# Regrouping the attention steps of a one-core decoder layer: probabilities times v one step later

## The chip, the cores and the metric

One core of one Trainium2 chip runs the whole layer as one program. The metric is the device time of an execution in microseconds; lower is better. The engines have short names here: PE is TensorE (its weight loads are PEld), DVE is VectorE, ACT is ScalarE, POOL is GpSimd, and SP is the queue that issues most transfers.

## What is computed

One decoder layer on a sequence of 512 rows and 1024 channels, all in 32-bit floats. Only the attention half of the first sub-layer matters here, with what stands right behind it:

```python
proj = rms_norm(h, mix_pre_g) @ w_in          # q, k, v, u, gv: 5 x 512 columns
attn_out = moba_attention(q, k, v)            # 8 heads x 64; with 512 rows all past blocks are selected: causal attention
gmlp_out = gmlp_spatial_gating(gelu(u), gelu(gv), ...)
mixed = concat([rms_norm(attn_out, attn_out_g), rms_norm(gmlp_out, gmlp_out_g)])
h = h + rms_norm(mixed @ w_o, mix_post_g)
hn = rms_norm(h, mlp_pre_g)                   # then w_up, squared relu, w_down, and the gated embedding
```

## The kernel before

The rows are cut into four tiles of 128 (`qt`, or `t`). Every large product is made of three matmuls in fp32r (high by high, high by low, low by high), so each weight slab and each activation is split into a high part by ACT (`w_hi`, line 935) and a low part by DVE (`w_lo`, line 440). A projection tile `proj(n)` is 24 matmuls of 512 columns in one PSUM bank. There is no planner: each engine runs a list that is written out by hand, and semaphores order the lists.

The attention runs in 16 steps, four row tiles times four pairs of heads; unit 4*qt + pair is one pair of one row tile. In a step PE does this, in this order:

1. `scores(step)`: six matmuls in fp32r, two heads side by side on 64 rows of the array each (lines 1607, 1611, 1612 with kT), into banks 3 and 4. It waits until ACT has read the scores of the step before (`probs_ready`).
2. `turn_probs(step - 1)`: full-array transposes of the probabilities (line 1754) into banks 5 and 6, qt + 1 for each head.
3. half a projection tile, 12 matmuls (lines 1607, 1611, 1612 with actT or mixT). Steps 4 and 5 make the two halves of tile 19 (v of the last rows); from step 6 on they are tiles of the output projection, whose second halves (the attention rows) wait for `attn_lo`.
4. `attend(step - 1)`: probabilities times v in plain fp32, two heads side by side on 64 columns of the array each (line 1774), into bank 7. It waits until DVE (`drain_pt0`, line 557) and ACT (`drain_pt1`, line 1073) have copied the transposes out.

Meanwhile DVE masks the scores, takes the maxima (`row_maxima`, lines 543, 548, 551) and copies out head 0; ACT does the exponentials (`softmax`, line 1064) and copies out head 1. In steps 0 to 2 and 5 to 8 both also split two weight slabs (`STEP_SPLITS`), and in steps 1, 3 and 5 ACT drains a tile of v (`proj_drain`, line 1021).

When a row tile is complete, a chain of small operations normalises it:

- `attn_inverse` (DVE, lines 564, 566): reciprocal of the row sums, spread over 512 columns of `attn`
- `turn_inverse` (PE, line 1661), `drain_inverse` (ACT, line 1078): transposed, and back into `attn`
- `attn_columns` (DVE, line 573): times bank 7
- `square_attn` (ACT, line 1086), `attn_sum` (DVE, line 578), `mean_square` (PE, line 1700, one column), `attn_mean` (DVE, line 583)
- one power on POOL (line 1454), `attn_spread` (DVE, line 588), `turn_scale` (PE, line 1705, in the middle of the projection), `attn_scale` (DVE, line 595), `attn_hi` (ACT, line 1090) and `attn_lo` (DVE, line 602)

Before the change the first three and the square stand in step 4*qt + 4, the sum and the mean in step 4*qt + 5, and the rest in step 4*qt + 6. The mean is written to bank 7.

Behind the last step come the remaining output projection (tiles 25 to 27), the residual (`add_mixed(t)`: DVE, two of line 615 and two of line 623), the square of the new h (`square_h1(t)`, ACT, line 969), its root on POOL (lines 1387, 1388), `norm_h1(t)` (ACT, line 1113) and the transposes `turn_hn` (PE, line 1661) for the MLP. Here ACT and DVE also split the four slabs of `w_ple` (lines 933 and 437) and then the first slabs of `w_up`. The raw slabs pass through a ring of two pairs: SP issues the load of a pair (line 1532) when DVE has made the low parts of the pair two before it. ACT's list there is: `square_h1(2)`, the split of the first `w_up` pair, `norm_h1(2)`, `square_out(3)`, the second pair, `hn_turn_hi(4)` and `(5)`, `square_h1(3)`, the third pair, `norm_h1(3)`; PE's `turn_hn(6)` waits for the last. PE's program for the whole layer is one fixed list too: what it loses in a wait is made up nowhere.

Of the kernel before, what the change touches and what calls it, by code (L numbers as in the profile page):

```python
# [39 lines left out]
P = 128  # L40
D = 1024
SEQ = 512
TT = SEQ // P
KD = D // P
W = 512
# [9 lines left out]
EPS = 1e-6  # L55
# [58 lines left out]
def phase_one_results():  # L114

    names = []
    for n in range(20):
        names.append(("proj", n))  # L120
        if n in (8, 9):
            names += [("mix", 2 * (n - 8)), ("mix", 2 * (n - 8) + 1)]
        if 9 <= n <= 16:
            names.append(("qkT", n - 9))
        if 12 <= n <= 15:
            names.append(("gateT", n - 12))
    names += [("proj", n) for n in range(20, 26)]
    first = {"proj": 0, "mix": BANK_S, "qkT": BANK_PT, "gateT": BANK_O}
    turns = {"proj": 3, "mix": 2, "qkT": 2, "gateT": 1}
    banks = {(kind, i): first[kind] + i % turns[kind] for kind, i in names}  # L130

    banks["proj", 3], banks["proj", 4], banks["proj", 5] = BANK_S, BANK_S + 1, BANK_PT
    a, b, c = (banks["proj", n] for n in (20, 21, 22))
    late = [(("attnT", 0), b), (("proj", 19), c), (("proj", 20), a), (("attnT", 1), c), (("proj", 21), b),
            (("proj", 22), c), (("attnT", 2), b), (("proj", 23), a), (("proj", 24), b),
            (("hT", 0), 5), (("hT", 1), 6), (("attnT", 3), 4), (("proj", 25), c), (("hT", 2), a), (("hT", 3), 6),
            (("proj", 26), 3), (("proj", 27), 4),
            (("ple", 0), 7), (("ple", 1), 6), (("ple", 2), 5), (("hT", 4), a), (("hT", 5), b),
            (("ple", 3), c), (("ple", 4), 7), (("ple", 5), 6), (("hT", 6), 3),
            (("hT", 7), 4), (("ple", 6), 5), (("ple", 7), a)]  # L140
    assert c == banks["proj", 19]
    banks.update(late)
    return names[:-7] + [name for name, _ in late], banks


def tail_results():
# [33 lines left out]
def hymba_layer(nc, x, xT, pT, weights, columns, rope, ws, rows, out):  # L180
# [6 lines left out]
    with ExitStack() as ctx:  # L187
# [237 lines left out]
        def _(dve):  # L425
# [154 lines left out]

            def attn_mean(qt):
                dve.wait_ge(mean_filled, qt + 1)
                nc.vector.tensor_scalar(mean_at[:, qt:qt + 1], psum[:, BANK_O, W - P:W - P + 1], EPS, None,
                                        ALU.add).then_inc(mean_ready, 1)

            def attn_spread(qt):
# [43 lines left out]
                        bank1["hT", i])  # L630

            for step in range(TT * PAIRS):
                if step >= 6 and step % 4 == 2:
                    attn_spread(step // 4 - 1)
                row_maxima(step)
                if step >= 1:
                    drain_pt0(step - 1)
                if step >= 4 and step % 4 == 0:
                    attn_inverse(step // 4 - 1)
                if step >= 5 and step % 4 == 1:  # L640
                    attn_sum(step // 4 - 1)
                if step >= 6 and step % 4 == 2:
                    attn_scale(step // 4 - 1)
                if step >= 6 and step % 4 == 2:
                    attn_lo(step // 4 - 1)
                for slab in STEP_SPLITS.get(step, ()):
                    splits(slab)
                if step >= 4 and step % 4 == 0:
                    attn_columns(step // 4 - 1)
                if step >= 5 and step % 4 == 1:  # L650
                    attn_mean(step // 4 - 1)
                if step == 11:
                    add_mixed(0)
                if step == 15:
                    add_mixed(1)
            drain_pt0(15)
            attn_inverse(3)
            hn_turn_lo(0)
            hn_turn_lo(1)
            attn_columns(3)  # L660
# [4 lines left out]
            hn_turn_lo(3)  # L665
            attn_scale(3)
            attn_lo(3)
            for i in range(2):
                splits(SLAB_PLE + 2 * i)
            add_mixed(2)  # L670
            dve.wait_ge(pT_hi_done, 1)
            nc.vector.tensor_tensor(pT_lo[:], pT_raw[:], pT_hi[:].bitcast(F32), ALU.subtract
                                    ).then_inc(pT_lo_done, 1)
# [250 lines left out]
        def _(act):  # L924
# [194 lines left out]


            for step in range(TT * PAIRS):
                if step >= 1:
                    drain_pt1(step - 1)
                softmax(step)
                if step >= 6 and step % 4 == 2:
                    attn_hi(step // 4 - 1)
                for slab in STEP_SPLITS.get(step, ()):
                    splits(slab)
                if step in (1, 3, 5):
                    proj_drain(17 + step // 2)  # L1130
                if step == 10:
                    square_out(0)
                if step == 12:
                    square_h1(0)
                    norm_h1(0)
                if step >= 4 and step % 4 == 0:
                    drain_inverse(step // 4 - 1)
                    square_attn(step // 4 - 1)
                if step == 14:
                    square_out(1)  # L1140
            drain_pt1(15)
            square_h1(1)
            hn_turn_hi(0)
            hn_turn_hi(1)
            norm_h1(1)
            drain_inverse(3)
            square_attn(3)
            act.wait_ge(pv_done, 16)
            act.dma_start(pT_raw[:], pT).then_inc(pT_loaded, 16)
# [451 lines left out]
        def _(pe):  # L1601
# [95 lines left out]

            def mean_square(qt):
                pe.wait_ge(at_summed, qt + 1)
                nc.tensor.matmul(psum[:, BANK_O, W - P:W - P + 1], at_rows[:], mean_of_w[:],  # L1700
                                 start=True, stop=True).then_inc(mean_filled, 1)

            def turn_scale(qt):
# [42 lines left out]
            def turn_probs(unit):  # L1746

                qt = unit // PAIRS
                pe.wait_ge(probs_ready, unit + 1)
                if unit == 0:  # L1750
                    pe.wait_ge(*drained["qkT", 2 * TT - 1])
                for s in range(2):
                    for k in range(qt + 1):
                        mm = nc.tensor.transpose(psum[:, BANK_PT + s, k * P:(k + 1) * P],  # L1754
                                                 probs[:, unit % 2, s, k * P:(k + 1) * P], ident[:])
                    mm.then_inc(pt_filled, 1)
# [20 lines left out]
                mm.then_inc(pv_done, 1)  # L1777

            for step in range(TT * PAIRS):
                scores(step)  # L1780
                if step >= 1:
                    turn_probs(step - 1)
                n, k0 = STEP_TILES[step]
                proj(n, range(k0, k0 + 2))
                if step in (6, 10, 14):
                    turn_scale(step // 4 - 1)
                proj(n, range(k0 + 2, k0 + 4))
                if step in (4, 8, 12):
                    turn_inverse(step // 4 - 1)
                if step >= 1:  # L1790
                    attend(step - 1)
                if step in (5, 9, 13):
                    mean_square(step // 4 - 1)
            turn_probs(15)
            proj(25, range(0, 4))
            pe.wait_ge(pt0_drained, TT * PAIRS)
            pe.wait_ge(pt1_drained, TT * PAIRS)
            turn_hn(0)
            turn_hn(1)
            turn_inverse(3)  # L1800
            attend(15)
            proj(25, range(4, 8))
            mean_square(3)
            turn_hn(2)
# [195 lines left out]
```

## Time and profile before

| | us |
|---|---|
| median of 3 runs (lowest, highest) | 615.1 (615.03, 616.13) |
| profiled execution, whole time | 614.93 |
| its span, first to last instruction | 613.2 |
| PE busy in the span | 600.3 (98%) |
| DVE, ACT, POOL busy | 403.8, 313.2, 82.5 |

The profiled execution lies 0.2 us under the median, and 1.7 us of it lie outside the span. A matmul of 512 columns is shown 0.39 us long, but the next one starts 0.23 us after it: they are pipelined, and their ends are modelled. So distances on PE are read from start to start. The attention steps run from about 109 to 190 us, and the MLP begins behind 222 us.

### The profile page before, as it was taken

Reading aid. Unit: us, or ns where it says so; the run is one execution under the profiler, and the core shown is the slowest. Engines: PE = TensorE matmul, PEld = TensorE weight load, DVE = VectorE, ACT = ScalarE, POOL = GpSimd, SP = SyncE. Lnnn points to the kernel's source line nnn. Section 1 sums busy time; section 2 is a strip of 40 time slices with the busy share of each in tenths; the row PEclk is TensorE's granted clock in tenths of the full one; section 3 lists DMA queues with packets and bytes.
Section 4 is the critical chain, followed back from the end, with each engine's and each line's share of the span. In section 5 each row is a group of like instructions: output and inputs, shape, how many; then the busy total and the mean of one; then the engine's idle time right before and its main releaser. Section 6 shows DMA issues by size and latency. Waiting matters only on the chain.

```text
span 613.2 us, 7823 instructions
## 1 busy us (share of the span) xinstructions
PE 600.3 (98%) x2922; PEld 489.4 (80%) x2922; DVE 403.8 (66%) x603; ACT 313.2 (51%) x541; POOL 82.5 (13%) x152
## 2 busy tenths in 40 slices
PE   8999999999999999999999999999999999999995
PEld 6888888777767878888888888888888888888884
DVE  5476444567755793766867757757778578668654
ACT  6754544656454755554534625544546355534422
POOL 1176332000001120001001001010010010001011
PEclk9999999999999999999999999999999999999998
DMA  8654332223000359554737556638365566234011
GB/s 309 253 195 141 105 103 69 68 69 104 1 2 26 110 181 322 139 210 93 190 137 158 137 156 153 220 75 201 138 134 145 160 151 210 93 130 168 13 69 69
DMA packets 23653, 82.90 MB, mean 135 GB/s; under 512 B 2752, under 2 KB 3136, under 8 KB 23104
## 3 DMA queue, kind: packets, MB, share of 16 engines
q1 hardware_dynamic: 18000, 60.83, 28.2%
q0 software_dynamic: 4032, 14.68, 14.0%
q10 hardware_dynamic: 1584, 6.90, 2.9%
q8 instruction: 23, 0.38, 0.2%
q14 instruction: 14, 0.11, 0.1%
HBM read 78.20 MB, written 4.19 MB: 134 GB/s over the span
## 4 chain that ended last, share of the span: by engine, by line
PE 88%; DVE 5%; ACT 3%; issue 1%; DMA 1%; POOL 1%; SPq 0%; DVEq 0%; ACTq 0%; POOLq 0%
PE psum L1607 28%; PE psum L1612 28%; PE psum L1611 28%; PE psum L1661 2%; PE psum L1774 1%; PE psum L1754 1%; DVE stat L548 1%; DMA first_raw_a<-weights_dram 1%; DVE w_lo L440 1%; ACT work L1113 1%; PE psum L1675 1%; ACT probs L1064 1%; ACT w_hi L935 0%; DVE psum L615 0%; DVE psum L543 0%
## 5 line engine op out<-in xcount | busy, mean ns | idle before, releaser
L440 DVE SCALAR_TENSOR_TENSOR w_lo<-raw,cols,w_hi 128x512 fp32r<-128x512 f32 x112 | 86.3, 813 | 46.7 <-ACT w_hi L935 46.5
L1612 PE MATMUL psum<-actT_hi,w_lo 128*128 128x512 f32 x256 | 99.8, 390 | 0.0
L1611 PE MATMUL psum<-actT_lo,w_hi 128*128 128x512 f32 x256 | 99.8, 390 | 0.0
L1607 PE MATMUL psum<-actT_hi,w_hi 128*128 128x512 f32 x256 | 99.7, 389 | 0.0
L935 ACT ACTIVATE w_hi<-raw,cols 128x512 fp32r<-128x512 f32 x112 | 74.3, 713 | 42.8 <-PE psum L1607 25.4
L1607 PE MATMUL psum<-w_hi,actT_hi 128*128 128x512 f32 (+1 forms) x232 | 90.6, 390 | 1.3 <-DVE w_lo L440 1.2
L1612 PE MATMUL psum<-w_hi,actT_lo 128*128 128x512 f32 (+1 forms) x232 | 88.7, 383 | 0.0
L1611 PE MATMUL psum<-w_lo,actT_hi 128*128 128x512 f32 (+1 forms) x232 | 88.7, 382 | 0.0
L1607 PE MATMUL psum<-t_hi,a_hi 128*128 128x512 f32 x212 | 83.6, 394 | 0.0
L1611 PE MATMUL psum<-t_lo,a_hi 128*128 128x512 f32 x212 | 83.6, 394 | 0.0
L1612 PE MATMUL psum<-t_hi,a_lo 128*128 128x512 f32 x212 | 83.6, 394 | 0.0
L764 DVE TENSOR_TENSOR acc<-acc,psum 128x512 f32<-128x512 f32 x90 | 58.4, 682 | 22.6 <-PE psum L1612 22.4
L1611 PEld LDWEIGHTS psum<-actT_lo,w_hi 128*128 128x128 f32 x256 | 48.1, 188 | 10.4
L1607 PEld LDWEIGHTS psum<-actT_hi,w_hi 128*128 128x128 f32 x256 | 48.1, 188 | 10.3
L1612 PEld LDWEIGHTS psum<-actT_hi,w_lo 128*128 128x128 f32 x256 | 48.0, 188 | 10.1
L1472 POOL DMA_DIRECT2D raw_x<-weights_dram x21 | 18.5, 883 | 259.4 <-DVE t_lo L705 259.4
L705 DVE TENSOR_TENSOR t_lo<-raw_x,t_hi 128x1024 fp32r<-128x1024 f32 x28 | 34.3, 1224 | 27.1 <-ACT t_hi L1195 27.1
L1607 PEld LDWEIGHTS psum<-w_hi,actT_hi 128*128 128x128 f32 x232 | 43.6, 188 | 10.2 <-DVE w_lo L440 1.9
L1612 PEld LDWEIGHTS psum<-w_hi,actT_lo 128*128 128x128 f32 x232 | 43.6, 188 | 8.6
L1611 PEld LDWEIGHTS psum<-w_lo,actT_hi 128*128 128x128 f32 x232 | 43.7, 188 | 7.9
L1195 ACT ACTIVATE t_hi<-raw_x 128x1024 fp32r<-128x1024 f32 x28 | 29.6, 1057 | 36.7 <-DMA raw_x<-weights_dram 27.2
L1612 PEld LDWEIGHTS psum<-t_hi,a_lo 128*128 128x128 f32 x212 | 39.8, 188 | 9.3
(169 smaller groups left out, 917.8 us busy)
## 6 DMA issues: line engine op xcount, KB each, us to landing
raw<-weights_dram SPq DMA_DIRECT2D x66, 512.0 KB, 3.6
raw_o<-weights_dram SPq DMA_DIRECT2D x23, 512.0 KB, 4.0
raw_x<-weights_dram POOLq DMA_DIRECT2D x21, 512.0 KB, 5.4
raw_x<-weights_dram SPq DMA_DIRECT2D x9, 512.0 KB, 5.4
raw_o<-weights_dram POOLq DMA_DIRECT2D x7, 512.0 KB, 9.0
ple_spill<-ple ACTq DMA_DIRECT2D x1, 2048.0 KB, 9.4
out_dram<-h SPq DMA_DIRECT2D x7, 256.0 KB, 2.0
xT_raw<-xT_dram SPq DMA_DIRECT2D x4, 256.0 KB, 5.8
```

The lines of the kernel that those rows point to most:

```text
L440: nc.vector.scalar_tensor_tensor(out=w_lo[:, place_at, :], in0=source, scalar=gain, in1=high, op0=ALU.mult, op1=ALU.subtract).then_inc(sla ...
L548: nc.vector.tensor_reduce(row_max, psum[:, BANK_S:BANK_S + 2, 0:n], AXIS_X, ALU.max).then_inc(max_found, 1)
L705: nc.vector.tensor_tensor(t_lo[n % T_RING][:], t_source(n), t_hi[n % T_RING][:].bitcast(F32), ALU.subtract).then_inc(t_lo_done, 1)
L764: nc.vector.tensor_tensor(part, part, bank, how).then_inc(product_added, 1)
L935: nc.scalar.activation(w_hi[:, place_at, :], source, ACT.Copy, scale=gain).then_inc(slab_hi, 1)
L1064: last = nc.scalar.activation(probs[:, unit % 2, s, 0:n], psum[:, BANK_S + s, 0:n], ACT.Exp, bias=neg_max[:, s:s + 1], scale=SCALE, accum_ ...
L1195: nc.scalar.activation(t_hi[n % T_RING][:], t_source(n), ACT.Copy).then_inc(t_hi_done, 1)
L1472: nc.gpsimd.dma_start(raw_x[step % 2][:], weights[down_in_stream(step, rows, half)], accum_op=ALU.add).then_inc(x_added, 16)
L1607: begin = nc.tensor.matmul(out, a_hi, b_hi, start=first, stop=False, skip_group_check=read_between)
L1611: nc.tensor.matmul(out, a_hi, b_lo, start=False, stop=False, skip_group_check=read_between)
L1612: return nc.tensor.matmul(out, a_lo, b_hi, start=False, stop=last, skip_group_check=read_between)
L1661: mm = nc.tensor.transpose(psum[:, banks[name], j * P:(j + 1) * P], source[:, j * P:(j + 1) * P], ident[:])
```

## The change

PE does `attend` for the unit two steps back, between the scores and the transposes, instead of for the last unit behind the projection. `turn_inverse` moves from the end of step 4*qt + 4 to the middle of step 4*qt + 5, between `attend` and `turn_probs`. `mean_square` moves from the end of step 4*qt + 5 to step 4*qt + 6, between the scores and `attend`; for the first three row tiles it now writes to column 0 of bank 5, and waits until DVE has read the transposes there; `turn_probs` in the same step waits until the mean is read. On ACT `drain_inverse` goes to the head of step 4*qt + 5, and `square_attn` behind the softmax, the splits and the `proj_drain` of that step. On DVE `attn_columns` and `attn_sum` are in step 4*qt + 5, and `attn_mean` stands ahead of the maxima of step 4*qt + 6. Behind the steps, `attend(15)` and `turn_inverse(3)` change places on PE, `drain_inverse(3)` goes ahead of `norm_h1(1)` on ACT, `attn_inverse(3)` ahead of `drain_pt0(15)` on DVE, and `add_mixed(2)` ahead of the splits of `w_ple` on DVE.

```diff
--- before.py
+++ after.py
@@ -141,6 +141,10 @@
     assert c == banks["proj", 19]
     banks.update(late)
     return names[:-7] + [name for name, _ in late], banks
+
+
+def mean_bank(qt):
+    return BANK_PT if qt < TT - 1 else BANK_O
 
 
 def tail_results():
@@ -580,7 +584,7 @@
 
             def attn_mean(qt):
                 dve.wait_ge(mean_filled, qt + 1)
-                nc.vector.tensor_scalar(mean_at[:, qt:qt + 1], psum[:, BANK_O, W - P:W - P + 1], EPS, None,
+                nc.vector.tensor_scalar(mean_at[:, qt:qt + 1], psum[:, mean_bank(qt), 0:1], EPS, None,
                                         ALU.add).then_inc(mean_ready, 1)
 
             def attn_spread(qt):
@@ -630,31 +634,31 @@
                         bank1["hT", i])
 
             for step in range(TT * PAIRS):
-                if step >= 6 and step % 4 == 2:
-                    attn_spread(step // 4 - 1)
+                qt, turn_of = step // 4 - 1, step % 4 if step >= 4 else -1
+                if turn_of == 2:
+                    attn_mean(qt)
                 row_maxima(step)
+                if turn_of == 2:
+                    attn_spread(qt)
                 if step >= 1:
                     drain_pt0(step - 1)
-                if step >= 4 and step % 4 == 0:
-                    attn_inverse(step // 4 - 1)
-                if step >= 5 and step % 4 == 1:
-                    attn_sum(step // 4 - 1)
-                if step >= 6 and step % 4 == 2:
-                    attn_scale(step // 4 - 1)
-                if step >= 6 and step % 4 == 2:
-                    attn_lo(step // 4 - 1)
+                if turn_of == 0:
+                    attn_inverse(qt)
+                if turn_of == 1:
+                    attn_columns(qt)
+                if turn_of == 2:
+                    attn_scale(qt)
+                    attn_lo(qt)
                 for slab in STEP_SPLITS.get(step, ()):
                     splits(slab)
-                if step >= 4 and step % 4 == 0:
-                    attn_columns(step // 4 - 1)
-                if step >= 5 and step % 4 == 1:
-                    attn_mean(step // 4 - 1)
+                if turn_of == 1:
+                    attn_sum(qt)
                 if step == 11:
                     add_mixed(0)
                 if step == 15:
                     add_mixed(1)
+            attn_inverse(3)
             drain_pt0(15)
-            attn_inverse(3)
             hn_turn_lo(0)
             hn_turn_lo(1)
             attn_columns(3)
@@ -665,9 +669,9 @@
             hn_turn_lo(3)
             attn_scale(3)
             attn_lo(3)
+            add_mixed(2)
             for i in range(2):
                 splits(SLAB_PLE + 2 * i)
-            add_mixed(2)
             dve.wait_ge(pT_hi_done, 1)
             nc.vector.tensor_tensor(pT_lo[:], pT_raw[:], pT_hi[:].bitcast(F32), ALU.subtract
                                     ).then_inc(pT_lo_done, 1)
@@ -1119,6 +1123,8 @@
 
 
             for step in range(TT * PAIRS):
+                if step >= 5 and step % 4 == 1:
+                    drain_inverse(step // 4 - 1)
                 if step >= 1:
                     drain_pt1(step - 1)
                 softmax(step)
@@ -1133,8 +1139,7 @@
                 if step == 12:
                     square_h1(0)
                     norm_h1(0)
-                if step >= 4 and step % 4 == 0:
-                    drain_inverse(step // 4 - 1)
+                if step >= 5 and step % 4 == 1:
                     square_attn(step // 4 - 1)
                 if step == 14:
                     square_out(1)
@@ -1142,8 +1147,8 @@
             square_h1(1)
             hn_turn_hi(0)
             hn_turn_hi(1)
+            drain_inverse(3)
             norm_h1(1)
-            drain_inverse(3)
             square_attn(3)
             act.wait_ge(pv_done, 16)
             act.dma_start(pT_raw[:], pT).then_inc(pT_loaded, 16)
@@ -1697,7 +1702,9 @@
 
             def mean_square(qt):
                 pe.wait_ge(at_summed, qt + 1)
-                nc.tensor.matmul(psum[:, BANK_O, W - P:W - P + 1], at_rows[:], mean_of_w[:],
+                if qt < TT - 1:
+                    pe.wait_ge(pt0_drained, 4 * qt + 5)
+                nc.tensor.matmul(psum[:, mean_bank(qt), 0:1], at_rows[:], mean_of_w[:],
                                  start=True, stop=True).then_inc(mean_filled, 1)
 
             def turn_scale(qt):
@@ -1749,6 +1756,8 @@
                 pe.wait_ge(probs_ready, unit + 1)
                 if unit == 0:
                     pe.wait_ge(*drained["qkT", 2 * TT - 1])
+                if unit >= 5 and unit % 4 == 1:
+                    pe.wait_ge(mean_ready, unit // 4)
                 for s in range(2):
                     for k in range(qt + 1):
                         mm = nc.tensor.transpose(psum[:, BANK_PT + s, k * P:(k + 1) * P],
@@ -1777,28 +1786,30 @@
                 mm.then_inc(pv_done, 1)
 
             for step in range(TT * PAIRS):
+                qt, turn_of = step // 4 - 1, step % 4 if step >= 4 else -1
                 scores(step)
+                if turn_of == 2:
+                    mean_square(qt)
+                if step >= 2:
+                    attend(step - 2)
+                if turn_of == 1:
+                    turn_inverse(qt)
                 if step >= 1:
                     turn_probs(step - 1)
                 n, k0 = STEP_TILES[step]
                 proj(n, range(k0, k0 + 2))
-                if step in (6, 10, 14):
-                    turn_scale(step // 4 - 1)
+                if turn_of == 2:
+                    turn_scale(qt)
                 proj(n, range(k0 + 2, k0 + 4))
-                if step in (4, 8, 12):
-                    turn_inverse(step // 4 - 1)
-                if step >= 1:
-                    attend(step - 1)
-                if step in (5, 9, 13):
-                    mean_square(step // 4 - 1)
+            attend(14)
             turn_probs(15)
             proj(25, range(0, 4))
             pe.wait_ge(pt0_drained, TT * PAIRS)
             pe.wait_ge(pt1_drained, TT * PAIRS)
             turn_hn(0)
             turn_hn(1)
+            attend(15)
             turn_inverse(3)
-            attend(15)
             proj(25, range(4, 8))
             mean_square(3)
             turn_hn(2)
```

## Rows read from the trace of the kernel before

**Rows 1.** The page, part 1: busy time and share of each engine.

```profile
PE 600.3 (98%) x2922; PEld 489.4 (80%) x2922; DVE 403.8 (66%) x603; ACT 313.2 (51%) x541; POOL 82.5 (13%) x152
```

**Rows 2.** Waits of PE: us in total, times, longest us.

```profile
PE psum L1774 <- DVE probsT L557: 1.4, 1, 1.4
...
PE psum L1661 <- ACT work L1113: 0.8, 1, 0.8
PE psum L1700 <- DVE at_rows L578: 0.4, 1, 0.4
PE psum L1661 <- DVE attn L566: 0.2, 1, 0.2
```

**Rows 3.** Timeline of PE, steps 4 and 5: start, us, line, op, count.

```profile
128.23 0.40 PE L1612 MATMUL psum<-w_hi,actT_lo 128*128 128x512 f32 x1
128.46 0.60 PE L1661 MATMUL psum<-ident,attn 128*128 128x128 f32 x4
128.99 0.44 PE L1774 MATMUL psum<-probsT,v 128*64 128x128 f32 x4
129.36 0.40 PE L1607 MATMUL psum<-kT_hi,mixT_hi 64*128 64x256 f32 x2
...
129.93 0.66 PE L1754 MATMUL psum<-ident,probs 128*128 128x128 f32 x4
...
132.95 0.39 PE L1612 MATMUL psum<-w_hi,actT_lo 128*128 128x512 f32 x1
133.27 0.66 PE L1774 MATMUL psum<-probsT,v 128*64 128x128 f32 x8
```

**Rows 4.** Timeline of PE at the start of step 1, and behind step 15.

```profile
112.58 0.39 PE L1612 MATMUL psum<-w_hi,actT_lo 128*128 128x512 f32 x1
112.92 0.34 PE L1607 MATMUL psum<-kT_hi,mixT_hi 64*128 64x128 f32 x2
...
188.34 1.09 PE L1774 MATMUL psum<-probsT,v 128*64 128x128 f32 x16
189.37 1.09 PE L1754 MATMUL psum<-ident,probs 128*128 128x128 f32 x8
```

**Rows 5.** Timeline of ACT and DVE: v's drain, and square and sum.

```profile
133.93 0.68 ACT L1021 ACTIVATE v<-psum,stat 128x512 f32<-128x512 f32 x1
...
197.12 0.63 ACT L1086 ACTIVATE junk<-attn 128x512 f32<-128x512 f32 x1 [0.83 <-DVE attn L573]
...
197.79 1.04 DVE L578 TENSOR_REDUCE at_rows<-junk 128x128 f32<-128x512 f32 x1 [0.70 <-ACT junk L1086]
```

**Rows 6.** Timeline: ends of softmax(7), softmax(9) on ACT; scores(8), (9) on PE.

```profile
142.94 0.20 ACT L1064 ACTIVATION_READ_ACCUMULATOR probs<-psum,stat 128x1 f32 x1
...
143.29 0.45 PE L1607 MATMUL psum<-kT_hi,mixT_hi 64*128 64x384 f32 x2
...
148.87 0.45 PE L1607 MATMUL psum<-kT_hi,mixT_hi 64*128 64x384 f32 x2
...
153.27 0.20 ACT L1064 ACTIVATION_READ_ACCUMULATOR probs<-psum,stat 128x1 f32 x1
```

**Rows 7.** Behind the steps: timelines of SP, DVE, ACT; sources L1532, L1387.

```profile
205.22 1.53 SPq L1532 DMA_DIRECT2D raw<-weights_dram  x2
...
DMA to landing us min/median/max: 3.2/3.2/4.0
...
206.17 1.41 DVE L615 SCALAR_TENSOR_TENSOR psum<-psum,stat,gain_post 128x512 f32<-128x512 f32 x2
207.49 1.28 DVE L623 TENSOR_TENSOR h<-h,psum 128x512 f32<-128x512 f32 x2
...
209.85 1.32 ACT L935 ACTIVATE w_hi<-raw,cols 128x512 fp32r<-128x512 f32 x2
...
L1387 POOL TENSOR_SCALAR stat<-stat x8: 190/190/629, 160.5 to 218.8; 128x1 f32<-128x1 f32 x8
...
220.09 1.15 ACT L1113 ACTIVATE work<-h,stat 128x1024 f32<-128x1024 f32 x1 [0.23 <-POOL stat L1388]
```

## Prediction

> **What bounds the kernel now.** I read the page first, then the waits of PE, then PE's timeline through the attention steps, then ACT and DVE beside it. The page shows PE busy for 98% of the span [rows 1]; nothing else is near. So the time is PE's list: what its instructions take, start to start, and what it waits. The change adds or removes no arithmetic, so only two things can move the time: the cost of passing from one kind of matmul to the next, and waits.
>
> There are four waits in the part that the change touches [rows 2]: 1.4 us before `attend(12)`, for `drain_pt0`; 0.2 before `turn_inverse(1)`; 0.4 before `mean_square(3)`; 0.8 before `turn_hn(6)`. Idle time is counted from a modelled end 0.39 after a start, while without a wait the next start would come 0.32 or 0.23 after it [rows 3], so each costs PE 0.07 (attend) or 0.16 more: 1.5, 0.4, 0.5 and 0.9 us.
>
> **Term 1, the passages: +0.2 us.** In the steps now, start to start [rows 3]: projection to `attend` 0.32 (132.95 to 133.27) where another projection matmul would follow after 0.23; `attend` to scores 0.37 for four records (128.99 to 129.36), where full streams give 0.1 for a pair of records, so about 0.15 is extra; scores to transposes 0.57 in all. Projection to `turn_inverse`, both on the full array but fp32r and fp32, is 0.23 (128.23 to 128.46): nothing extra. So a passage costs some 0.1 (and stretches the first matmul behind it by 0.05 to 0.1) where the shape changes that the matmuls take of the array, and nothing where only the number type changes. In the old order a step has three such passages: full to 64 columns, 64 columns to 64 rows, 64 rows to full. In the new order it has full to 64 rows, 64 rows to 64 columns, 64 columns to full: three again. Two of the new ones occur in the trace [rows 4]: projection to scores 0.34 (112.58 to 112.92), and `attend` to transposes, 1.03 for 16 records, or eight pairs of 0.1 and about 0.2 extra. That is 0.02 more than projection to `attend`, and equal to `attend` to scores. Scores to `attend` occurs nowhere; between nothing at all (a gain of 0.15 in 14 steps, 2.1 us) and twice the dearest passage (2.1 us lost) it is nearest to `attend` to scores, the same two shapes the other way, and I take the same price. 14 steps x 0.02 = 0.3, less a little where `turn_inverse` now spares the transposes their stretch: +0.2. The mean and the inverse sit among neighbours of other shapes before and after, one extra passage for each mean both times: 0.
>
> The Trainium skill, in TensorEngine Tiling (Array Packing), Tiling Modes, Key Properties, says that changing the tiling mode drains TensorE. By that rule alone, with three changes of mode before and after, this term would be 0 and not 0.2; the trace agrees with it in that fp32r to fp32 on the full array shows no cost.
>
> **Term 2, waits that go: -1.9 us.** `attend(12)` waited for a drain that DVE did late, because in step 13 the inverse's product stood ahead of the maxima, and ACT had come to it only behind `square_h1(0)` and `norm_h1(0)`. It now follows the drain by a whole projection half, some 2.6 us: -1.5. What is late next there is the mean, term 4. `turn_inverse(1)` now has scores and `attend` ahead of it, over 1 us more than the 0.4 that it lacked: -0.4.
>
> **Term 3, a new wait in step 6: +1.9 us.** `mean_square(0)` needs `attn_sum(0)`, which needs `square_attn(0)`, and that now stands on ACT behind `proj_drain(19)`. Tile 19 is what PE makes in step 5 itself. Count from the start of the last matmul of step 5. ACT can drain the tile 0.43 later (0.39 of the matmul and a hand-over of 0.04); in the rows it began 1.0 behind the matmul only because the splits were in front of it. The drain takes 0.68, the square 0.63, the sum 1.04, with 0.04 between engines [rows 5] and 0.1 of overlap on ACT: 0.43 + 0.58 + 0.63 + 0.04 + 1.04 + 0.05 = 2.8. PE without a wait is there after 0.34 to the scores and 0.57 through them: 0.9. So PE stands still for 1.9. Behind the waiting matmul in PE's queue is everything: `attend(4)`, the transposes, the projection. On DVE `attn_mean` now waits ahead of `row_maxima(6)`, so the maxima too go with it, the scores of step 7 have 2.6 us of projection to cover that, and nothing more is lost in step 6. The splits on DVE end 1.2 behind the last matmul, in front of the sum but not in its way. Bounds: 1.7 to 2.1.
>
> **Term 4, smaller waits: +0.8 us.** Before, scores(8) began 0.15 behind the end of softmax(7) (142.94 + 0.20, against 143.29) [rows 6]: there is no slack in the loop of maxima, softmax and splits, and with the chain of the mean moved into step 6's maxima it starts a little later. I take 0.3 for scores(8) and (9), between 0 and 0.6. For `mean_square(1)`: softmax(9) ended at 153.47 [rows 6], a bit later now (+0.1) as `drain_inverse` is ahead of it; then square and sum as above, 1.65, give 155.2. PE, from scores(9) at 148.87 [rows 6], passes scores 0.7, `attend` 0.6, inverse 0.5, transposes 0.6, projection 2.6 + 0.34, scores 0.7: 154.9. Wait 0.35, between 0 and 0.7. Step 13 is longer on PE (four blocks of keys, not three) and so is its softmax: 0.1, between 0 and 0.6.
>
> **Term 5, behind the steps: +0.9 us.** Two moves. First, `drain_inverse(3)` waits for transposes that are now behind `attend(15)` and `norm_h1(1)` is between it and the square, so `mean_square(3)` comes 0.2 later. ACT's load of `pT_raw` is issued behind that square and goes 0.2 later too; it has 5 us of cover. Second and larger, `add_mixed(2)` goes ahead of the four low parts of `w_ple`. It takes 2.6 (206.17 to 207.49 + 1.28) [rows 7]. PE needs these parts only with the first `ple` tile, covered. But SP's next load waits for them: its pair, issued at 205.22, is now issued at 205.22 + 2.6 + 0.1 = 207.9 (the mean's delay is in it), and lands 3.2 to 4.0 later [rows 7], at 211.1 at the earliest. ACT split this pair at 209.85; behind the split stand `norm_h1(2)`, `square_out(3)`, and with them the roots, `add_mixed(3)`, `square_h1(3)` and `norm_h1(3)` at 220.09, for which PE's `turn_hn(6)` waited already. All that moves by 1.3; of this 0.4 may come back, since one POOL step in that chain took 0.63 and not 0.19 [rows 7]. So +0.9 in PE, which holds the mean's 0.2, as these would have run beside each other. Bounds: 0.5 (the POOL step and a quick landing) to 1.8 (4.0 to land). If the load is not what comes last, the earlier `add_mixed(2)` instead brings the chain forward, by about 0.5.
>
> **Sum.** 0.2 - 1.9 + 1.9 + 0.8 + 0.9 = +1.9. On the profiled execution's 614.93 that is 616.8; the median of the runs is 0.2 above it, so I say 617.0.
>
> **The rivals.**
> - **The late load costs nothing.** ACT's split of `w_up` then starts in time, and the last wait shrinks by 0.5, while the mean's 0.2 stays: the sum without term 5 is +1.0, and 1.0 + 0.2 - 0.5 = +0.7 gives 615.8, the same as before within noise. For it: loads of 512 KB land in 3.2. Against it: the issue waits for DVE by program order, and 207.9 + 3.2 is behind 209.85 whatever the queue does.
> - **Scores to `attend` is free.** Then 2.1 less, 614.9: no change. For it: both are small shapes. Against it: `attend` to scores costs 0.2 [rows 3].
> - **The type of number is what costs, not the shape.** Faster. The old order changes between fp32r and fp32 four times in a step, the new one twice, since `attend` and the transposes stand together. If the 0.15 at projection to `attend`, the 0.2 at `attend` to scores and the 0.15 at scores to transposes were this, only one of the three would be left: 14 x 0.35 = 4.9 less and 612.1. It decides from 0.13 a step on (1.9 / 14). Against it stand the 0.23 of projection to `turn_inverse` and the 0.34 of projection to scores, fp32r on both sides.
> - **The wait in step 6 spreads.** If the late maxima make the scores of steps 7 to 9 wait longer than I took, or a landing takes 4.0, up to 2 us come on top: 619.
>
> **How the numbers follow.** A difference of 0.2%, 1.2 us, is about what a measurement can tell here. My sum 0.5; the spreading wait 0.12; the late load free 0.14; scores to `attend` free or cheap 0.1; the number types 0.05; other gains 0.09 (a wait in step 6 that is shorter with term 5 small). Slower by over 0.2%: nearly all of the first two, 0.60. Same: 0.27. Faster: 0.13. The range must reach from the cheap passages, 614.5, to the high ends of terms 4 and 5 together, 618.8. The sum's own range is 616.0 to 618.2.
>
> **What would show it.** In the profile after: a wait of PE before line 1700 of about 1.7 us (1.9 by starts) in step 6, for DVE's sum; none before `attend(12)`; scores to `attend` 0.2 to 0.3 behind the last scores; the distance between the second low part of `w_ple` and its load unchanged, ACT idle for the transfer before its split of `w_up`, and `turn_hn(6)` idle for some 1.7 us instead of 0.8. It is wrong if ACT does not reach the square behind `proj_drain(19)`, if the load lands before ACT is there, or if new passages differ from 0.1.

## The result and the profile after

The changed kernel took 618.25 us (median of 6 runs, 616.84 to 619.07) against 615.07 (6 runs) before: a ratio of 1.0047, interval 1.0031 to 1.0064. It is slower by 3.2 us; 617.0 was forecast, in a range of 614.5 to 618.8. The profiled execution took 619.07 with a span of 617.3, 4.1 more than before.

The page, part 1, of the kernel after answers to [rows 1]:

```profile
PE 602.8 (98%) x2922; PEld 490.7 (79%) x2922; DVE 403.0 (65%) x603; ACT 312.3 (51%) x541; POOL 84.3 (14%) x152
```

As many instructions as before, and PE at 98% as before: the page alone tells nothing of what happened. The waits of PE do (answering to [rows 2]). Left out are waits at the start of the program, where the kernels are the same: 1.6 us before line 1719, and those before line 1612 for `w_lo` (line 1607 in the kernel before), 1.2 in all in the profile before, 1.0 here and 0.5 to 1.9 in the others of this study. They are one source of the spread between executions: `scores(0)` starts anywhere from 108.9 to 110.2 us.

```profile
PE psum L1707 <- DVE at_rows L582: 2.7, 3, 1.8
...
PE psum L1666 <- ACT work L1117: 1.5, 1, 1.5
...
PE psum L1612 <- DVE ple L684: 0.2, 1, 0.2
PE psum L1612 <- ACT probs L1068: 0.2, 1, 0.2
```

Line 1707 is the mean, which waited once and now waits three times by this view (a fourth wait, of step 14, shows only start to start). The waits before `attend(12)` and `turn_inverse(1)` are gone. The last transposes of h (1666) wait twice as long. Two lines are new.

The passages, in PE's timeline of step 5 after, against [rows 3] and [rows 4]:

```profile
128.84 0.39 PE L1617 MATMUL psum<-w_hi,actT_lo 128*128 128x512 f32 x1
129.16 0.40 PE L1612 MATMUL psum<-kT_hi,mixT_hi 64*128 64x256 f32 x2
...
129.51 0.29 PE L1617 MATMUL psum<-kT_hi,mixT_lo 64*128 64x256 f32 x2
129.72 0.44 PE L1783 MATMUL psum<-probsT,v 128*64 128x128 f32 x4
130.09 0.66 PE L1666 MATMUL psum<-ident,attn 128*128 128x128 f32 x4
130.59 0.60 PE L1763 MATMUL psum<-ident,probs 128*128 128x128 f32 x4
```

Projection to scores is 0.32 (128.84 to 129.16), the same as projection to `attend` before; scores to `attend` is 0.21 (129.51 to 129.72), where `attend` to scores was 0.20 from the last of its four records. Three passages a step, each at the old price.

Now step 6, the place of the forecast wait. ACT, DVE and PE from their timelines:

```profile
133.96 0.69 ACT L1025 ACTIVATE v<-psum,stat 128x512 f32<-128x512 f32 x1 [0.17 <-PE psum L1617]
134.55 0.62 ACT L1090 ACTIVATE junk<-attn 128x512 f32<-128x512 f32 x1
...
135.20 1.02 DVE L582 TENSOR_REDUCE at_rows<-junk 128x128 f32<-128x512 f32 x1 [0.57 <-ACT junk L1090]
...
134.20 0.29 PE L1617 MATMUL psum<-kT_hi,mixT_lo 64*128 64x256 f32 x2
136.27 0.38 PE L1707 MATMUL psum<-mean_of_w,at_rows 128*128 128x1 f32 x2 [1.78 <-DVE at_rows L582]
136.58 0.95 PE L1783 MATMUL psum<-probsT,v 128*64 128x128 f32 x8
137.46 1.12 PE L1763 MATMUL psum<-ident,probs 128*128 128x128 f32 x4
138.23 0.78 PE L1612 MATMUL psum<-w_hi,mixT_hi 128*128 128x512 f32 x1
138.80 0.63 PE L1616 MATMUL psum<-w_lo,mixT_hi 128*128 128x512 f32 x1
139.23 0.63 PE L1617 MATMUL psum<-w_hi,mixT_lo 128*128 128x512 f32 x1
...
140.62 0.27 PE L1712 MATMUL psum<-ident,at_rows 128*128 128x128 f32 x1
```

Drain of tile 19, square, sum, mean: a chain without a gap, as worked out, and PE stands still from 134.20 + 0.21 (where the mean would start without a wait) to 136.27, 1.85 us. But look at what follows. The projection matmuls start 0.43 apart, not 0.23, and are 0.63 long. The windows of PE, with the granted clock behind the busy time, show why:

```profile
133.50:136.20 2.70, 0.99 (x8) 1.00 0.20 38
136.50:140.40 3.90, 3.90 (x20) 0.56 0.24 95
140.60:144.00 3.40, 3.40 (x27) 1.00 0.01 2
```

The columns are the stretch, its length, PE's busy time (instructions), the granted clock, the DMA share and GB/s. Behind the wait the clock was granted at 0.56 of full over 3.9 us, that is at 1.2 GHz instead of 2.4 for 3.4 us of it. From the mean to `turn_scale` it is 4.35 us (136.27 to 140.62).

Behind the steps, from the timelines of SP, ACT and PE, against [rows 7]:

```profile
210.59 1.52 SPq L1537 DMA_DIRECT2D raw<-weights_dram  x2
...
213.96 1.34 ACT L939 ACTIVATE w_hi<-raw,cols 128x512 fp32r<-128x512 f32 x2 [3.55 <-DMA raw<-weights_dram]
...
224.21 1.15 ACT L1117 ACTIVATE work<-h,stat 128x1024 f32<-128x1024 f32 x1 [0.23 <-POOL stat L1393]
...
221.59 0.40 PE L1617 MATMUL psum<-w_hi,pT_lo 128*128 128x512 f32 x1
222.22 0.50 PE L1612 MATMUL psum<-w_hi,pT_hi 128*128 128x512 f32 x1 [0.24 <-DVE ple L684]
...
223.50 0.39 PE L1617 MATMUL psum<-w_hi,pT_lo 128*128 128x512 f32 x1
225.41 0.33 PE L1666 MATMUL psum<-ident,work 128*128 128x128 f32 x1 [1.52 <-ACT work L1117]
```

ACT stood idle for 3.55 us until the load of the first `w_up` pair landed. The wait before `turn_hn(6)` is 1.9 - 0.23 = 1.7 us where it was 0.9, and 0.4 is new before the sixth `ple` tile (`ple_tile(5)`), whose bank DVE empties behind the late `add_mixed(3)`.

The account of the 4.1 us between the two profiled executions, all by starts on PE. It is of one execution of each kernel; the profiled one of the changed kernel is its slowest, with a mean clock of 0.995.

| | us |
|---|---|
| before scores(0), the kernels are the same there: chance | +0.3 |
| scores(2) waits for softmax(1), new | +0.27 |
| `mean_square(0)` | +1.85 |
| half clock behind it, 4.35 against 2.79 without | +1.6 |
| scores(8) and (9), 0.42 and 0.41 behind the projection instead of 0.32 | +0.2 |
| `mean_square(1)`, `mean_square(2)` | +0.4, +0.03 |
| waits before `attend(12)` and `turn_inverse(1)`, gone | -1.9 |
| `mean_square(3)`, 0.72 instead of 0.54 | +0.2 |
| `ple_tile(5)` and `turn_hn(6)` | +0.4, +0.75 |
| sum | 4.1 |

### The profile page after: what moved, and what is told of

Same layout as the page of the kernel before. It is cut to its first block, busy times and chain, and to the rows that moved or that the text cites. A ratio compares the mean times of both kernels' runs of the same rounds, so it can differ in the third digit from the quotient of the medians.

```text
span 617.3 us, 7829 instructions
## 1 busy us (share of the span) xinstructions
PE 602.8 (98%) x2922; PEld 490.7 (79%) x2922; DVE 403.0 (65%) x603; ACT 312.3 (51%) x541; POOL 84.3 (14%) x152
## 4 chain that ended last, share of the span: by engine, by line
PE 92%; DVE 3%; ACT 2%; DMA 1%; issue 1%; POOL 0%; SPq 0%; DVEq 0%; ACTq 0%; POOLq 0%
PE psum L1612 29%; PE psum L1617 28%; PE psum L1616 28%; PE psum L1666 2%; PE psum L1783 2%; PE psum L1763 1%; DVE w_lo L444 1%; DMA first_raw_a<-weights_dram 1%; DVE stat L552 1%; PE psum L1680 1%; ACT probs L1068 1%; DVE at_rows L582 1%; ACT w_hi L939 0%; ACT work L1117 0%; DVE psum L547 0%
```

## The experiments

The kernel before ran beside them: 614.99 us (31 runs) with the first four, 615.00 (35 runs) with the last four. The mean clock of a run is the granted clock over its whole span. Even in the profiles without a loss inside the work it is 0.996 to 0.998, as the clock falls to half behind PE's last matmul (it was granted at 0.67 over the last 5.2 us of the profile before); 3.4 us at half clock take another 0.003 off.

### The square ahead of the splits and of the drain of tile 19

```diff
 # ACT
                 softmax(step)
+                if step >= 5 and step % 4 == 1:
+                    square_attn(step // 4 - 1)
...
                     norm_h1(0)
-                if step >= 5 and step % 4 == 1:
-                    square_attn(step // 4 - 1)
 # DVE
                     attn_columns(qt)
+                    attn_sum(qt)
                 for slab in STEP_SPLITS.get(step, ()):
                     splits(slab)
-                if turn_of == 1:
-                    attn_sum(qt)
```

> The changed kernel, but ACT does the square right behind the softmax of its step, ahead of the splits and of the drain of tile 19, and DVE does the sum ahead of its splits. Theory A, the wait in step 6 is the square queued behind the drain of tile 19: the wait of PE before the mean of the first row tile goes (1.85 us), the waits of the two later means stay within 0.1 of 0.4 and 0.03, and the granted clock stays whole, since no idle stretch of 2 us is left: 614.9 to 615.4, with the slow members of the runs (619) gone. Rival B, it is the product, the sum or the new place of the mean itself that comes late: a wait of over 1 us stays, 617 or more. Rival C, the clock's stretch at half speed has nothing to do with the wait: the wait goes, but some runs still lie 1.7 us above the others.

Measured: 615.48 (615.06 to 616.41, 11 runs), ratio to before 1.0005 (0.9996 to 1.0014); none of the runs had a mean clock under 0.996. From its PE timeline:

```profile
134.63 0.29 PE L1616 MATMUL psum<-kT_hi,mixT_lo 64*128 64x256 f32 x2
134.84 0.38 PE L1706 MATMUL psum<-mean_of_w,at_rows 128*128 128x1 f32 x2
135.16 0.66 PE L1782 MATMUL psum<-probsT,v 128*64 128x128 f32 x8
136.17 0.52 PE L1762 MATMUL psum<-ident,probs 128*128 128x128 f32 x3 [0.36 <-DVE stat L587]
```

The mean follows the scores after 0.21: its wait is gone. That is theory A, and the median is 2.8 us under the changed kernel's. Against the three runs of the changed kernel with a mean clock of 0.998, whose median is 616.88, it is 1.4 less: the 1.85 less the new 0.4. A smaller wait took its place, not forecast: the transposes wait 0.4 until DVE has read the mean from their bank, because `attn_mean` is now behind the splits of step 5 on DVE. At 615.48 the time is 0.1 above the forecast.

### The residual addition back behind the splits

```diff
 # DVE
-            add_mixed(2)
             for i in range(2):
                 splits(SLAB_PLE + 2 * i)
+            add_mixed(2)
```

> The changed kernel with the third residual addition back behind the splits of the embedding weights on DVE. Theory A, the late load: ACT splits the first pair for the MLP in time, PE's waits before the last transposes of h and before the fifth embedding tile shrink from 1.7 and 0.4 us (start to start, less the 0.23 of a stream) to 0.9 and 0: 1.1 to 1.2 us less than the changed kernel, at equal clock. Rival B, the wait grew because the mean of the last row tile is later, or because POOL's root took 2.2 us there: 0 to 0.3 less.

Measured: 616.73 (615.79 to 619.41, 12 runs), ratio to before 1.0028 (1.0016 to 1.0039). PE waited before the transposes of h as it did in the kernel before, and not at all before the `ple` tile:

```profile
PE psum L1666 <- ACT work L1117: 0.8, 1, 0.8
```

The runs fall into two groups: six from 615.79 to 616.41 with a mean clock of 0.996 or 0.997, six from 617.05 to 619.41 with 0.992 to 0.994. The changed kernel does the same: 616.84 to 617.89 at 0.998, 618.61 to 619.07 at 0.995. Group by group it is 1.0 and 1.7 less, by only three runs of the changed kernel in each; 1.1 to 1.2 was expected at equal clock, and the two places on PE show 1.2 less (1.17 against 1.91 before the transposes, nothing against 0.4 before the `ple` tile). Theory A stands. Its profiled execution was of the upper clock, with the same idle stretch before the mean; there the way from the mean to `turn_scale` is 2.79, the number used in the account above. So the idle stretch does not bring the half clock every time:

```profile
136.50 0.38 PE L1707 MATMUL psum<-mean_of_w,at_rows 128*128 128x1 f32 x2 [1.78 <-DVE at_rows L582]
...
139.28 0.27 PE L1712 MATMUL psum<-ident,at_rows 128*128 128x128 f32 x1
```

### One pair of splits ahead of the addition, one behind

```diff
 # DVE
+            splits(SLAB_PLE)
             add_mixed(2)
-            for i in range(2):
-                splits(SLAB_PLE + 2 * i)
+            splits(SLAB_PLE + 2)
```

> The changed kernel with the first pair of the embedding weights split ahead of the residual addition and the second behind it, so that the load of the first pair for the MLP is issued as early as in the old order, while the addition still comes 1.2 us sooner than there. Theory A, the load alone was what came late: the wait before the last transposes of h becomes smaller than before the change, 0.4 to 0.9 us: 1.2 to 1.6 us less than the changed kernel. Rival B, the load's turn in the queue does not matter and the addition's early place is what hurts: no less than in the changed kernel, 1.7.

Measured: 617.37 (615.55 to 618.61, 12 runs), ratio 1.0028 (1.0017 to 1.0039). Again two groups, five from 615.55 to 616.57 (clock 0.995 to 0.997) and seven from 617.35 to 618.61 (0.993 to 0.995). By their medians they lie 0.8 and 1.5 under those of the changed kernel, where 1.2 to 1.6 was expected. ACT no longer waits for the load, but for POOL:

```profile
211.15 1.32 ACT L939 ACTIVATE w_hi<-raw,cols 128x512 fp32r<-128x512 f32 x2
213.50 1.15 ACT L1117 ACTIVATE work<-h,stat 128x1024 f32<-128x1024 f32 x1 [1.03 <-POOL stat L1393]
```

So the load was what came late, and with it on time the earlier addition is worth next to nothing: PE's wait is 0.7 here and 0.8 with the old order. What may have taken the addition's gain stands in the timelines of DVE and POOL:

```profile
211.18 1.22 DVE L676 TENSOR_TENSOR pT_lo<-pT_raw,pT_hi 128x1024 fp32r<-128x1024 f32 x1
211.40 1.04 POOL L1392 TENSOR_SCALAR stat<-stat 128x1 f32<-128x1 f32 x1 [5.48 <-ACT junk L973]
212.53 0.94 POOL L1393 TENSOR_TENSOR stat<-stat 128x1 f32<-128x1 f32 x1
```

The two POOL operations took 1.04 and 0.94 here, 0.19 and 0.55 with the old order: 1.24 more, about as much as the addition was to be sooner. No run took this away, so it is not shown as the cause; the last section says what it coincides with.

### The wait filled with matmuls

```diff
 # PE, mean_square
+                if qt == 0:
+                    pe.wait_ge(attn_ready, 1)
+                    for _ in range(20):
+                        nc.tensor.matmul(psum[:, BANK_O, 0:P], ident_bf[:], ident_bf[:], start=True, stop=True)
                 pe.wait_ge(at_summed, qt + 1)
```

> The changed kernel with 20 matmuls of 128 columns in bf16 (results overwritten, not used) in front of the wait for the first sum, so that PE is not idle in it; at 0.06 to 0.11 us each they take 1.2 to 2.1 us of a wait of 1.85. Theory A, the stretch at half clock in step 6 follows from the idle 2 us: it is gone in every run; the time is that of the better runs of the changed kernel, 616.8 to 617.2, or 0.3 more if the matmuls outlast the wait. Rival B, the clock falls whatever PE does in the wait, or by chance: the runs stay split, some at 619.

Measured: 616.92 (616.56 to 617.93, 8 runs), ratio 1.003 (1.002 to 1.0041); the mean clock was 0.996 to 0.998 in all. PE's timeline and the windows of the wait and of the stretch behind it:

```profile
133.87 1.29 PE L1707 MATMUL psum<-ident_bf 128*128 128x128 bf16 x20
135.73 0.38 PE L1711 MATMUL psum<-mean_of_w,at_rows 128*128 128x1 f32 x2 [0.57 <-DVE at_rows L582]
```
```profile
133.00:135.70 2.70, 2.16 (x28) 1.00 0.19 33
135.90:139.80 3.90, 3.90 (x27) 1.00 0.26 102
```

The mean is as late as in the changed kernel, but PE worked for 1.3 us of the wait, and the clock stayed whole: in the profile, and by the mean clock in all eight runs, where the changed kernel lost it in three of six and the two kernels above, with the same idle stretch, in about half of theirs. The wait itself costs its 1.85; the half clock behind it is a second price that comes of being idle, theory A.

### Both repairs

The edits of the first and the third experiment in one kernel.

> Both repairs in one kernel: the square right behind the softmax, and the first pair of the embedding weights split ahead of the residual addition. If the two faults are separate places of PE's list, their gains add up: the first repair gave 615.5, the second removes 1.2 at its place (waits of 0.9 instead of 1.7 + 0.4), so 614.2 to 614.5, 0.5 to 0.8 faster than before the change. Rival: the waits trade against each other (what the first repair gives is waited away at the second): 615.3 or more.

Measured: 614.46 (614.29 to 615.02, 11 runs), ratio 0.9984 (0.997 to 0.9999), clock 0.996 to 0.998. The two gains add up: 1.0 less than the first alone. It is 0.5 under the kernel before by the medians.

### One edit of the change in the kernel before

The kernel before, with `add_mixed(2)` ahead of the splits, the reverse of the second experiment's edit.

> The kernel before with one edit of the change alone: the third residual addition ahead of the splits of the embedding weights. Theory A, the late load costs this by itself: PE's wait before the last transposes of h grows by 0.8 and a wait of about 0.3 appears before the fifth embedding tile, 616.0 to 616.3, no other wait moves. Rival B, it only hurts together with the later mean of the last row tile: 614.8 to 615.2.

Measured: 616.12 (615.55 to 617.95, 12 runs), ratio 1.0022 (1.0012 to 1.0032). The late load does it by itself:

```profile
210.41 1.34 ACT L935 ACTIVATE w_hi<-raw,cols 128x512 fp32r<-128x512 f32 x2 [3.43 <-DMA raw<-weights_dram]
```
```profile
218.18 0.39 PE L1612 MATMUL psum<-w_hi,pT_lo 128*128 128x512 f32 x1
218.69 0.50 PE L1607 MATMUL psum<-w_hi,pT_hi 128*128 128x512 f32 x1
...
219.95 0.39 PE L1612 MATMUL psum<-w_hi,pT_lo 128*128 128x512 f32 x1
221.87 0.33 PE L1661 MATMUL psum<-ident,work 128*128 128x128 f32 x1 [1.53 <-ACT work L1113]
```

1.92 before the transposes instead of 1.16, and 0.51 before the `ple` tile instead of 0.23: +1.0, and 1.1 in the medians. No other wait of the attention part moved. Two of the twelve runs (617.48 and 617.95) had a mean clock of 0.994.

### The last square ahead of the norm

```diff
 # ACT, on top of both repairs
             drain_inverse(3)
-            norm_h1(1)
             square_attn(3)
+            norm_h1(1)
```

> The kernel with both repairs, and the square of the last row tile ahead of the norm of h on ACT. The inverse of that row tile is still transposed behind the products, so its mean comes at about the old time or a little sooner: that wait falls from 0.72 to some 0.1 to 0.5. If the norm then comes too late for the next transposes of h, the wait only moves there and the time stays that of the kernel with both repairs; else 0.3 to 0.5 less: 613.8 to 614.3.

Measured: 614.44 (613.97 to 615.45, 12 runs), ratio 0.999 (0.9981 to 0.9999). The expectation failed: the wait before `mean_square(3)` only went from 0.72 to 0.66. What holds this mean is not the square's place on ACT but that its transposes are behind `attend(15)`: from the start of `turn_inverse(3)` at 195.10 over ACT's copy (195.79), DVE's product (196.49), the square (197.22) and the sum (197.88) to the mean at 199.01 no engine waits for anything else, and with the norm ahead of the square this was only 0.07 longer. This and the kernel with both repairs are the quickest here, 0.5 to 0.6 us or 0.1% under the kernel before, at the edge of what was measured.

### Two more transposes in each step

```diff
 # PE, on top of the last kernel, behind the projection half
+                if step >= 1:
+                    pe.wait_ge(pt0_drained, step)
+                    for _ in range(2):
+                        nc.tensor.transpose(psum[:, BANK_PT, 3 * P:4 * P], ident[:], ident[:])
```

> The last kernel with two more fp32 transposes on the full array (results overwritten, not used) behind the projection half of each of 15 steps, between two groups of fp32r matmuls. Theory A, only the shape that matmuls take of the array costs a passage: each step grows by two transposes of 0.11, 0.22, in all 3.3. Rival B, the type of number costs too (0.1 for each way and 0.1 of stretch): 0.4 to 0.45 a step, in all 6 to 6.7.

Measured: 616.25 (616.09 to 616.82, 11 runs), 1.8 more than without them. PE's timeline:

```profile
133.66 0.39 PE L1616 MATMUL psum<-w_hi,actT_lo 128*128 128x512 f32 x1
133.90 0.38 PE L1806 MATMUL psum<-ident 128*128 128x128 f32 x2
134.21 0.40 PE L1611 MATMUL psum<-kT_hi,mixT_hi 64*128 64x256 f32 x2
```

From the projection (fp32r) to the transposes (fp32) it is 0.23 (0.24 by the rounded starts), what the next projection matmul would take, and from the first of two transposes to the scores 0.31: 0.54 in all where 0.32 stood, 0.22 more a step, two transposes of 0.11. The type of number costs nothing. Fifteen steps make 3.3; the median rose by less because the waits before scores(2), (8), (9) and the first two later means, 1.0 together, and half of the 0.4 behind the splits vanished under the added work. What is left, 0.3, has no cause shown.

## Why the prediction was right, and where it was short

**Term 1, passages, +0.2.** Measured 0: projection to scores is 0.32 in most steps, not the 0.34 of the one row that I had [rows 4], and scores to `attend` has the price of the reverse. The bounds of plus and minus 2.1 were not needed. The Trainium skill's rule (TensorEngine Tiling (Array Packing), Tiling Modes, Key Properties: a change of the tiling mode drains TensorE), by which the term was 0, agrees: three changes of mode a step before and after, each at about 0.1 here. The rivals of the free passage and of the number types fell, the second by a run of its own.

**Term 2, waits that go, -1.9.** Both went; that is read from the trace alone, no run puts them back.

**Term 3, the wait in step 6, +1.9.** Measured 1.85, with the chain as worked out, and shown by the run that took the square out of the queue. What the step missed is the clock: it took PE to be as quick behind the wait as ahead of it, without giving a reason. In the profile PE went on at 1.2 GHz for 3.4 us, 1.6 us more, and half of the six runs show a mean clock lower by 0.003, as much as such a stretch takes off. Of the three kernels with an idle stretch of 1.85 in step 6, 3 of 6, 6 of 12 and 8 of 12 runs had a mean clock of 0.995 or less (one of the last eight, 616.57, has the time of the better ones); of the five kernels with neither that stretch nor the 1.4 us of idle before `attend(12)` (square first, wait filled, both repairs, the last square, the two transposes), none of 53. The two kernels that keep the wait before `attend(12)` had it too, the kernel before in 9 of 66 runs beside the experiments and the one with the addition moved in 2 of 12. Where in a run the clock fell is seen only in the two profiles of the lower clock, of the changed kernel and of the third experiment, and in both it is step 6; that it is `attend(12)` in the old order is not shown. This is what lies between 617.0 and 618.25: the three runs at the whole clock have their median at 616.88.

**Term 4, smaller waits, +0.8.** Measured 0.6: 0.2 for scores(8) and (9), 0.4 and 0.03 for the means. One was not seen: scores(2) now comes 0.37 sooner, as no `attend` is ahead of it, and softmax(1) is not done. Every step's loop was taken from step 6 on; steps 1 and 2 have splits as well.

**Term 5, behind the steps, +0.9.** Measured 1.35: 0.2 for the mean, 0.4 and 0.75 for `ple_tile(5)` and `turn_hn(6)`. The mechanism, the load behind the splits, is shown twice, by the edit taken out of the changed kernel and by the edit alone in the kernel before. The load was issued 2.6 late against PE's list and landed 3.4 behind its issue (210.59 to 213.96), so the chain moved by the 1.3 that I had worked out. The size was low because I let 0.4 of it come back in a late POOL step, which took 0.63 again, as in every profile of this study. It is no lone delay: it ended 0.05 behind the DVE split that was running when it began, and that split moves with the chain.

**The sum.** +1.9 was forecast; the better half of the runs at 616.84 to 617.89 shows +1.8 to +2.8, all of them +3.2. Without the clock and the chance at the start the terms measure +2.2. That this is so near is in part luck: terms 1 and 4 were 0.2 too high each, term 5 0.45 too low, and scores(2), 0.3, was not in the sum. That 618.25 lies in the range is luck as well: its upper end was drawn for late scores and a late landing, and the half clock stood nowhere in it.

## What to carry to other kernels

When a step is moved later, list what it then stands behind on its engine, and ask which of that waits for the very work that it was moved past: a square behind the drain of the tile that PE was making cost 1.85 us, and moving it ahead of that drain and of the splits gave back all but a new 0.4. A split that frees a ring slot is also the issue of a load: work put ahead of it delays the load by its own length, and the cost shows one transfer and several engines later. Where PE is the bound, count a wait of nearly 2 us at more than its length: in about half of the runs here it cost 1.6 us on top.

## What was not expected of the hardware

The granted clock fell to half for 3.4 us behind 1.85 us of idle time in both profiles of the lower clock, and by the mean clock in about half of 30 runs. Of the 53 runs of kernels with neither this idle stretch nor that before `attend(12)` none shows it; 1.3 us of small bf16 matmuls in the wait were enough to keep it.

A POOL operation can take many times its usual length while DVE works. The one on a single column (line 1392, 0.19 us as a rule) took 2.25 us behind `square_h1(2)` in the profile after, 1.04 in the four kernels with one pair of splits on either side of the addition, 0.51 in the kernels with the square first, with the wait filled and with the addition moved alone, and 0.19 in the kernel before and with the addition put back:

```profile
210.56 2.25 POOL L1392 TENSOR_SCALAR stat<-stat 128x1 f32<-128x1 f32 x1 [4.27 <-ACT junk L973]
...
211.55 1.22 DVE L676 TENSOR_TENSOR pT_lo<-pT_raw,pT_hi 128x1024 fp32r<-128x1024 f32 x1
```

DVE's operation ended at 212.77, POOL's at 212.81. It is so in all ten profiles. From 100 us on they hold 210 of POOL's small `TENSOR_SCALAR`s on `stat`. The 48 that took 0.47 us or more all began while DVE ran an operation with two inputs from SBUF (a low part `w_lo` or `pT_lo`, or a sum into `h`), and all ended 0.05 to 0.08 behind the end of a DVE operation of this kind. The other 162 took under 0.3; with them DVE was idle or read one input from PSUM. This is read from the traces; no run changes it alone, and why the one of 2.25 outlasted the two splits that ended in its time is not seen. In the changed kernel it cost nothing, as ACT waited for the load until 213.96 anyway; in the third experiment `norm_h1(2)` waited 1.03 for the slow pair.
